# Two edits of order in a hybrid streaming encoder: the PSUM bank of the small columns, and what VectorE and ScalarE do first in the merge

## Chip, cores and metric

The kernel runs on one core of a Trainium2 chip. The metric is the time of one execution on the device, in microseconds, as the median of several runs. The profile is of one further execution.

## The reference, cut to what matters

Two layers of an encoder for 512 prompt frames and 64 sample frames (T = 576 columns), width 1024, float32. Each layer is a token mixer and a gated MLP with a short convolution; what the change touches is the mixer:

```python
(a_q, a_k, a_v, i_q, i_k, i_w, b_q, b_k, b_v, c_q, c_k, c_v, c_f) = jnp.split(xn @ w_in, points, axis=-1)
c_logf = jax.nn.log_sigmoid(c_f + b_f)
# three attentions: A sparse (indexer i_q, i_k, i_w picks keys), B stick-breaking, C forgetting (c_logf)
branch = jnp.einsum('btnw,nwd->btnd', o, w_branch)
gate = jax.nn.sigmoid((xn @ w_gate).reshape(B, T, N_BRANCH, D_MODEL))
return jnp.einsum('btnd,btnd->btd', gate, branch) @ w_out
```

The "small columns" are a_v (64), i_w (4) and c_f (8): 76 columns of the projection that are narrower than a tile and go together.

## The kernel before, in words

Activations lie transposed: 128 features on the partitions, 576 frames in the free dimension, eight such tiles for the width of 1024. Each operand of a product is split in a high and a low part (wh and wl of the weights, xh and xl of the activations), and a product is three matmuls (high-high, high-low, low-high) for each half of 288 frames. One output tile over 1024 inputs is 48 matmuls.

Weights come in units of 512 KB into two raw buffers. A unit is two chunks of 512 columns. For each chunk ScalarE makes the high part (`high_part`, L455) and VectorE the low part (`low_part`, L798), into one of four slots. A high part waits until TensorE has finished the chunk four before it (semaphore `chunks`), TensorE waits for the low part (`low_done`), and SyncE loads the next unit when both low parts of a unit are made.

Output tiles go in turn to two PSUM buffers of two banks each, `dbank[0]` and `dbank[1]` (called bank 0 and bank 1 here). Each use has a number `d`; its bank is `d % 2`. TensorE begins use d when `dfree[d % 2]` says that the use before it in that bank has been taken out by VectorE. The uses at the start of a layer are D_KI = 0 (keys of branch A and of the indexer), D_IQ0 = 1 (index query, first tile; the second goes to another PSUM tensor, `ab`), D_SMALL = 2, and D_PASSED = 3, a use without a product, which TensorE marks as done itself so that the next use, D_Q[B] = 4, falls in bank 0. Nothing is planned at run time: each engine has a list of instructions in the order in which its Python code writes them, and runs it in that order.

TensorE's order at the start of a layer (L1477 on) is: keys, index query 0, index query 1, small columns (L1488), first half of query tile 0 of branch B (L1491), five transposes of the small columns (L1497), second half of that query tile (L1499), first half of the next (L1500), eight small products for the forget logits (L1505, L1506), second half (L1507), and then the index heads (L1517). VectorE's order is: take the keys (L818), take index query 0 (L820), low part 8, take index query 1 (L956), copies for the samples, low part 9, rotate the keys (L829 to L832), copy them (L965), low part 10, take the small columns (L969), copy a row of rstd into them (L971, which frees the bank), low part 11, rotate index query 0, low part 12, extract the turned small columns (L979 to L986), take query tile 0 (L820), and on to the forget logits (L995, L996). ScalarE makes the high parts and four partition-shifting copies for each rotation (L461).

The merge follows each branch's attention, in the order B, C, A (so six times in two layers). TensorE multiplies the branch's output o (split in oh and ol) by w_branch, eight tiles j = 0 to 7 in turn in the two banks. `branch_first` (L1425) does tiles 0 and 1, interleaved so that the high products of both come ahead of the low ones: the last 8 matmuls of tile 0, then the rest of tile 1, whose last 8 matmuls end it. Tiles 2 to 7 go through `dense` (L1370). VectorE multiplies tile j by gate j (L1216 in branch B, L1218 in C and A), which frees the bank, and in C and A adds the result to z (L1220). The gates are made by ScalarE and VectorE during the attention: VectorE takes the projection (L904), ScalarE makes abs, exp and ln (`gate_ln`), VectorE subtracts (`gate_sub`, L909), ScalarE makes the final exp (`gate_exp`, L494). The eighth gate (number 7) is finished at the start of the merge.

Of the kernel before, what the change touches and what calls it, by code (L numbers as in the profile page):

```python
# [40 lines left out]
HEADS = 8  # L41
# [16 lines left out]
B, C, A = 0, 1, 2  # L58
# [4 lines left out]
U_BR = {B: 24, C: 48, A: 64}  # L63
# [7 lines left out]
RAW_SLOTS = 2  # L71


D_KI, D_IQ0, D_SMALL, D_PASSED = range(4)
D_Q = {B: 4, C: 37, A: 70}
D_V = {B: 8, C: 41}
D_K = {B: 9, C: 42}
# [56 lines left out]
def encoder(nc, xT, w, const, masks, par, ki_past, v_past, bc_k_past, bc_v_past, lf_past,  # L134
            y, o_ki, o_k, o_v, o_av, o_lf, o_conv):
    with ExitStack() as ctx:
# [85 lines left out]
        def sem(name):  # L222
            return ctx.enter_context(nc.semaphore(name))
# [7 lines left out]
        dfree = [sem("dfree0"), sem("dfree1")]  # L231
# [30 lines left out]
        def chunks_done(l, n):  # L262

            return l * CHUNKS + SPLIT_SLOTS + n

        def freed(l, d):

            return START + l * (D_USES // 2) + d // 2
# [5 lines left out]
        def wait_taken(eng, l, d):  # L274

            eng.wait_ge(dfree[d % 2], freed(l, d) + 1)
# [155 lines left out]
        def _(act):  # L432
# [3 lines left out]
            def high_parts(l, upto, at_chunk=None):  # L436

                while split[0] <= upto:
                    c = split[0]
                    high_part(l * CHUNKS, l * (UNITS // 2), c)  # L440
                    split[0] += 1

            def high_part(before, units_before, c, in_half=0):
                v_ = c // 2
                if c % 2 == 0:

                    act.wait_ge(landed[v_ % 2], 16 * (units_before + v_ // 2 + 1))

                act.wait_ge(chunks, before + c + 1)
                stored = raw[v_ % 2][:, (c % 2) * 512:(c % 2) * 512 + 512]  # L450
                if v_ + in_half in TURNED_UNITS:
                    act.activation(as_turned(wh[:, c % SPLIT_SLOTS, :], 0), as_stored(stored, 0), ACT.Copy)
                    act.activation(as_turned(wh[:, c % SPLIT_SLOTS, :], 1), as_stored(stored, 1), ACT.Copy).then_inc(high_done, 1)
                else:
                    act.activation(wh[:, c % SPLIT_SLOTS, :], stored, ACT.Copy).then_inc(high_done, 1)  # L455
# [18 lines left out]
            def round_z(l, kk):  # L474

                act.wait_ge(z_ready, l * KD + kk + 1)
                act.activation(xh[:, kk, :], z[:, kk, :], ACT.Copy).then_inc(xh_ready, 1)

            def gate_ln(l, m, h):

                wait_taken(act, l, D_G[m] + 2 * h)
                part = tmp[:]
                act.activation(part, g[:, h, :], ACT.Abs).then_inc(act_steps, 1)
                steps[0] += 1
                act.wait_ge(act_steps, l * ACT_STRIDE + steps[0])
                act.activation(part, part, ACT.Exp, scale=-1.0).then_inc(act_steps, 1)
                steps[0] += 1
                act.wait_ge(act_steps, l * ACT_STRIDE + steps[0])
                act.activation(part, part, ACT.Ln, bias=1.0).then_inc(gate_lns, 1)

            def gate_exp(l, m, h):

                act.wait_ge(gate_subs, l * 24 + 8 * m + h + 1)
                act.activation(g[:, h, :], g[:, h, :], ACT.Exp).then_inc(gates_ready, 1)  # L494
# [14 lines left out]
            for l in range(LAYERS):  # L509
# [31 lines left out]
                for m in (B, C, A):  # L541
# [157 lines left out]
                        gate_exp(l, m, 2 * p)  # L699
                    high_parts(l, cg + 7)  # L700
                    gate_ln(l, m, HEADS - 1)
                    gate_exp(l, m, HEADS - 1)

                    for j in range(KD):

                        high_parts(l, 2 * U_BR[m] + j + 4)
                        if m == A and j:
                            round_z(l, j - 1)

# [67 lines left out]
        def _(dve):  # L777
# [4 lines left out]
            def step(ins):  # L782

                ins.then_inc(dve_steps, 1)
                steps[0] += 1
# [4 lines left out]
            def low_part(before, c, in_half=0):  # L790
                dve.wait_ge(high_done, before + c + 1)
                stored = raw[(c // 2) % 2][:, (c % 2) * 512:(c % 2) * 512 + 512]
                highs, lows = wh[:, c % SPLIT_SLOTS, :].bitcast(F32), wl[:, c % SPLIT_SLOTS, :]
                if c // 2 + in_half in TURNED_UNITS:
                    dve.tensor_tensor(as_turned(lows, 0), as_stored(stored, 0), as_turned(highs, 0), ALU.subtract)
                    dve.tensor_tensor(as_turned(lows, 1), as_stored(stored, 1), as_turned(highs, 1), ALU.subtract).then_inc(low_done, 1)
                else:
                    dve.tensor_tensor(lows, stored, highs, ALU.subtract).then_inc(low_done, 1)  # L798

            def low_parts(l, upto):  # L800
                while split[0] <= upto:
                    low_part(l * CHUNKS, split[0])
                    split[0] += 1
# [86 lines left out]
            def split_low(l, m, p):  # L890

                dve.wait_ge(oh_ready, l * 12 + 4 * m + p + 1)
                dve.tensor_tensor(ol[:, p, :], q[:, p, :], oh[:, p, :].bitcast(F32), ALU.subtract).then_inc(ol_ready, 1)  # L893
# [12 lines left out]
            def gate_sub(l, m, h):  # L906

                dve.wait_ge(gate_lns, l * 24 + 8 * m + h + 1)
                dve.scalar_tensor_tensor(g[:, h, :], g[:, h, :], 0.0, tmp[:], ALU.min, ALU.subtract).then_inc(gate_subs, 1)  # L909
# [36 lines left out]
            for l in range(LAYERS):  # L946
# [95 lines left out]
                for m in (B, C, A):  # L1042
# [162 lines left out]
                        for p in range(PAIRS - 1):  # L1205
                            split_low(l, m, p)
                    split_low(l, m, PAIRS - 1)
                    gate_sub(l, m, HEADS - 1)

                    for j in range(KD):  # L1210
                        low_parts(l, 2 * U_BR[m] + j + 4)
                        d = D_BR[m] + j
                        dve.wait_ge(chunks, chunks_done(l, 2 * U_BR[m] + j + 1))
                        dve.wait_ge(gates_ready, l * 24 + 8 * m + j + 1)
                        if m == B:
                            dve.tensor_tensor(z[:, j, :], dv[d % 2], g[:, j, :], ALU.mult).then_inc(dfree[d % 2], 1)  # L1216
                        else:
                            dve.tensor_tensor(g[:, j, :], dv[d % 2], g[:, j, :], ALU.mult).then_inc(dfree[d % 2], 1)  # L1218
                            dve.wait_ge(dfree[d % 2], freed(l, d) + 1)
                            ins = dve.tensor_tensor(z[:, j, :], z[:, j, :], g[:, j, :], ALU.add)  # L1220
                            if m == A:
                                ins.then_inc(z_ready, 1)
                                if j % 2:
                                    low_x(l, 1, j - 1)
                            else:
                                step(ins)
# [130 lines left out]
        def _(pe):  # L1357
            def dense(before, lo_wait, c0, outs, rh, rl, kks, begin=True, end=True):

                for n, kk in enumerate(kks):  # L1360
                    c = c0 + n // 4
                    if n % 4 == 0:

                        pe.wait_ge(low_done, before + c + 1)
                    lo_wait(kk)
                    a = (n % 4) * P
                    hi_w, lo_w = wh[:, c % SPLIT_SLOTS, a:a + P], wl[:, c % SPLIT_SLOTS, a:a + P]
                    for w_, r_, first, last in ((hi_w, rh, True, False), (hi_w, rl, False, False), (lo_w, rh, False, True)):
                        for half in range(2):
                            ins = pe.matmul(outs[half], w_, r_[:, kk, HALF * half:HALF * half + HALF],  # L1370
                                            start=first and n == 0 and begin, stop=last and n == len(kks) - 1 and end)
                    if n % 4 == 3 or n == len(kks) - 1:
                        ins.then_inc(chunks, 1)
# [23 lines left out]
            def project(l, u, d, wait=no_wait):  # L1397
                pe.wait_ge(dfree[d % 2], freed(l, d))
                dense(l * CHUNKS, wait, 2 * u, dhalf[d % 2], xh, xl, range(KD))
# [77 lines left out]
            for l in range(LAYERS):  # L1477
                project(l, U_KI, D_KI, xn_wait(l, 0))
                project(l, U_IQ, D_IQ0)
                if l == 0:  # L1480
                    dense(l * CHUNKS, no_wait, 2 * (U_IQ + 1), iq1_out, xh, xl, range(4), True, False)
                    pe.wait_ge(s_const, 16)
                    norm_sum(1)
                    dense(l * CHUNKS, no_wait, 2 * (U_IQ + 1) + 1, iq1_out, xh, xl, range(4, KD), False, True)
                else:
                    norm_sum(1 + 2 * l)
                    dense(l * CHUNKS, no_wait, 2 * (U_IQ + 1), iq1_out, xh, xl, range(KD))
                project(l, U_SMALL, D_SMALL)  # L1488
                wait_taken(pe, l, D_IQ0)
                pe.sem_inc(dfree[D_PASSED % 2], 1)  # L1490
                project_half(l, U_Q[B], D_Q[B], 0)  # L1491

                wait_taken(pe, l, D_SMALL)
# [539 lines left out]
```

## Time and profile before

| | |
|---|---|
| median of 3 runs | 2167.99 us (2167.51 to 2168.78) |
| the profiled execution | 2157.28 us |
| its span | 2155.4 us |
| TensorE busy | 2125.5 us, 99% |
| TensorE's weight loads busy | 2012.8 us, 93% |
| VectorE busy | 1341.5 us, 62% |
| ScalarE busy | 992.1 us, 46% |
| GpSimd busy | 187.8 us, 9% |
| mean granted TensorE clock | 0.997 of full speed |
| mean DMA rate | 81 GB/s |

The span goes from the first instruction to the last; the execution's own time has a little more around it. Busy times of one engine are the union of its instructions; matmuls are pipelined, so one lasts longer than the distance to the next. L971 is line 971 of the kernel before.

### The profile page before, as it was taken

To read this page: it belongs to the slowest core of one execution; us is meant where nothing else is said; L and a number is where in the kernel's file an instruction comes from. 1 tells how busy PE (TensorE), PEld (TensorE's weight loads), DVE (VectorE), ACT (ScalarE), POOL (GpSimd) and SP (SyncE) were. 2 spreads that over 40 slices of the span, in tenths; PEclk is the share of its full clock that TensorE was granted. 3 is DMA by queue.
4 is the path that set the end of the run, shared out by engine and by line. 5 is a ranking of instruction groups with operands and counts; after the bars stand their busy time and mean duration, and the time that the engine had idled before them with its cause. 6 is when DMAs were issued, how large, how long until landed. Compare 5 with 4: busy or idle time off the path is not lost.

```text
span 2155.4 us, 40042 instructions
## 1 busy us (share of the span) xinstructions
PE 2125.5 (99%) x16142; PEld 2012.8 (93%) x16142; DVE 1341.5 (62%) x2537; ACT 992.1 (46%) x1611; POOL 187.8 (9%) x138
## 2 busy tenths in 40 slices
PE   7999999999999999999999999999999999999998
PEld 7898998898899999999988989888989999999998
DVE  6668646766556773566465785377766476536653
ACT  5347414646626652344342672255465366424431
POOL 0000000000031110011300100000000301001112
PEclk9999999999999999999999999999999999999999
DMA  5231223121122222222232212231211222222222
GB/s 186 77 104 40 72 85 113 40 79 50 50 80 88 79 87 91 86 88 88 89 105 78 94 40 94 73 99 53 71 50 60 79 88 79 88 89 78 88 80 94
DMA packets 53493, 175.06 MB, mean 81 GB/s; under 512 B 6705, under 2 KB 11393, under 8 KB 53361
## 3 DMA queue, kind: packets, MB, share of 16 engines
q1 hardware_dynamic: 46896, 158.88, 23.9%
q0 software_dynamic: 2688, 9.95, 1.2%
q10 hardware_dynamic: 3776, 4.34, 0.6%
q8 instruction: 99, 1.62, 0.3%
q14 instruction: 34, 0.27, 0.0%
HBM read 160.25 MB, written 12.90 MB: 80 GB/s over the span
## 4 chain that ended last, share of the span: by engine, by line
PE 94%; DVE 3%; ACT 2%; issue 1%; DMA 0%; ACTq 0%; SPq 0%; DVEq 0%
PE d L1370 61%; PE d L1420 14%; PE ab L1466 4%; PE ab L1698 2%; PE d L1750 2%; PE d L1741 2%; PE d L1611 1%; PE d L1470 1%; PE ab L1691 1%; PE ab L1728 1%; DVE ol L893 1%; PE d L1431 0%; PE ab L1517 0%; PE d L1864 0%; PE ab L1548 0%
## 5 line engine op out<-in xcount | busy, mean ns | idle before, releaser
L455 ACT ACTIVATE wh<-raw 128x512 fp32r<-128x512 f32 x548 | 345.1, 631 | 736.9 <-PE d L1370 611.2
L798 DVE TENSOR_TENSOR wl<-raw,wh 128x512 fp32r<-128x512 f32 x548 | 379.9, 695 | 367.3 <-ACT wh L455 358.5
L1370 PE MATMUL d<-xh,wh 128*128 128x288 f32 x2400 | 517.4, 296 | 16.9 <-DVE z L971 8.5
L1370 PE MATMUL d<-xl,wh 128*128 128x288 f32 x2400 | 514.7, 295 | 0.0
L1370 PE MATMUL d<-xh,wl 128*128 128x288 f32 x2400 | 514.4, 295 | 0.0
L1370 PEld LDWEIGHTS d<-xh,wh 128*128 128x128 f32 x2400 | 385.8, 189 | 20.9 <-issue 10.6
L1370 PEld LDWEIGHTS d<-xl,wh 128*128 128x128 f32 x2400 | 385.7, 189 | 0.0
L1370 PEld LDWEIGHTS d<-xh,wl 128*128 128x128 f32 x2400 | 385.7, 189 | 0.0
L1420 PE MATMUL d<-xh,wh 128*128 128x288 f32 x768 | 173.3, 307 | 0.5 <-DVE g L904 0.5
L1420 PE MATMUL d<-xh,wl 128*128 128x288 f32 x768 | 164.5, 295 | 0.0
L1420 PE MATMUL d<-xl,wh 128*128 128x288 f32 x768 | 164.4, 295 | 0.0
L1370 PE MATMUL d<-al,wh 128*128 128x288 f32 x682 | 145.4, 294 | 0.0
L1370 PE MATMUL d<-ah,wh 128*128 128x288 f32 x682 | 145.3, 294 | 0.0
L1370 PE MATMUL d<-ah,wl 128*128 128x288 f32 x682 | 145.3, 294 | 0.0
L1420 PEld LDWEIGHTS d<-xh,wh 128*128 128x128 f32 x768 | 122.3, 189 | 3.9 <-DVE g L904 1.0
L1420 PEld LDWEIGHTS d<-xl,wh 128*128 128x128 f32 x768 | 123.2, 188 | 0.0
L1420 PEld LDWEIGHTS d<-xh,wl 128*128 128x128 f32 x768 | 123.0, 188 | 0.0
L410 POOL TENSOR_TENSOR al<-at,ah 128x576 f32 x44 | 63.9, 1451 | 652.6 <-ACT ah L740 652.6
L1274 DVE TENSOR_TENSOR hb<-d,rstd 128x512 f32<-128x512 f32 x88 | 60.9, 692 | 88.8 <-PE d L1370 88.8
L1370 PEld LDWEIGHTS d<-ah,wh 128*128 128x128 f32 x682 | 108.9, 188 | 0.0
L1370 PEld LDWEIGHTS d<-ah,wl 128*128 128x128 f32 x682 | 108.9, 188 | 0.0
L1370 PEld LDWEIGHTS d<-al,wh 128*128 128x128 f32 x682 | 108.8, 188 | 0.0
(319 smaller groups left out, 3236.4 us busy)
## 6 DMA issues: line engine op xcount, KB each, us to landing
raw<-in_w SPq DMA_DIRECT2D x288, 512.0 KB, 3.5
out_o_k<-k POOLq DMA_DIRECT2D x4, 1152.0 KB, 7.3
out_o_v<-v POOLq DMA_DIRECT2D x4, 1024.0 KB, 8.9
x<-in_xT SPq DMA_DIRECT2D x8, 288.0 KB, 6.6
out_y<-z SPq DMA_DIRECT2D x16, 144.0 KB, 1.9
k<-in_bc_k_past ACTq DMA_DIRECT2D x4, 512.0 KB, 5.0
v<-in_bc_v_past ACTq DMA_DIRECT2D x4, 512.0 KB, 6.2
w<-in_masks SPq DMA_DIRECT2D x1, 800.0 KB, 6.5
```

Of the source, the lines that this page charges most:

```text
L410: pool.tensor_tensor(al[:, bass.ds(i, 1), :].rearrange("p a n -> p (a n)"), at[:], ah[:, bass.ds(i, 1), :].rearrange("p a n -> p (a n)").b ...
L455: act.activation(wh[:, c % SPLIT_SLOTS, :], stored, ACT.Copy).then_inc(high_done, 1)
L798: dve.tensor_tensor(lows, stored, highs, ALU.subtract).then_inc(low_done, 1)
L893: dve.tensor_tensor(ol[:, p, :], q[:, p, :], oh[:, p, :].bitcast(F32), ALU.subtract).then_inc(ol_ready, 1)
L1274: dve.tensor_tensor(hb[:, s, 2:514], hv[:, 0:512], rstd[:, 0:512], ALU.mult)
L1370: ins = pe.matmul(outs[half], w_, r_[:, kk, HALF * half:HALF * half + HALF], start=first and n == 0 and begin, stop=last and n == len(kks) ...
L1420: ins = pe.matmul(dhalf[d][half], w_, r_[:, kk, HALF * half:HALF * half + HALF], start=first and kk == 0, stop=last and kk == KD - 1)
L1466: pe.matmul(o, x_[:, kk, t * P:t * P + P], w_[:, c % SPLIT_SLOTS, cols:cols + n], start=first and f_ and starts(t), stop=last and l_, skip ...
L1470: ins = pe.matmul(src(4), xp[:, kk, :], w_[:, c % SPLIT_SLOTS, cols:cols + n], start=first and f_ and starts(4), stop=last and l_, skip_gr ...
L1698: pe.matmul(ab[:, bank + i, a:a + n], q[r, p, t * P:(t + 1) * P], keys(r, p)[:, 0:n], start=a == 0, stop=False, skip_group_check=True)
L1741: ins = pe.transpose(spare[:, o + n:o + n + P], w1[:, a + n:a + n + P], ident)
L1750: pe.matmul(spare[r, t * P:(t + 1) * P], val(2 * p + i, kt), w2[:, w:w + P], start=first, stop=kt == t, skip_group_check=True)
```

## The change

Two things. D_SMALL and D_PASSED change places, so that the small columns go to bank 1 and the passed use is in bank 0; TensorE marks the passed use ahead of the small columns, when the keys have been taken (use 0, bank 0). In the merge, VectorE multiplies tile j by its gate ahead of low part j + 4 instead of behind it. The subtraction for gate 7 moves behind the product of tile 0 (VectorE), and the exponential for gate 7 moves behind the first high part of the merge (ScalarE). No instruction is added or taken away.

```diff
-D_KI, D_IQ0, D_SMALL, D_PASSED = range(4)
+D_KI, D_IQ0, D_PASSED, D_SMALL = range(4)
@@ ScalarE
                     gate_ln(l, m, HEADS - 1)
-                    gate_exp(l, m, HEADS - 1)
 
                     for j in range(KD):
 
                         high_parts(l, 2 * U_BR[m] + j + 4)
+                        if j == 0:
+                            gate_exp(l, m, HEADS - 1)
                         if m == A and j:
                             round_z(l, j - 1)
@@ VectorE
                     split_low(l, m, PAIRS - 1)
-                    gate_sub(l, m, HEADS - 1)
 
                     for j in range(KD):
-                        low_parts(l, 2 * U_BR[m] + j + 4)
                         d = D_BR[m] + j
                         dve.wait_ge(chunks, chunks_done(l, 2 * U_BR[m] + j + 1))
                         dve.wait_ge(gates_ready, l * 24 + 8 * m + j + 1)
@@ 
                             dve.tensor_tensor(z[:, j, :], dv[d % 2], g[:, j, :], ALU.mult).then_inc(dfree[d % 2], 1)
                         else:
                             dve.tensor_tensor(g[:, j, :], dv[d % 2], g[:, j, :], ALU.mult).then_inc(dfree[d % 2], 1)
+                        if j == 0:
+                            gate_sub(l, m, HEADS - 1)
+                        low_parts(l, 2 * U_BR[m] + j + 4)
+                        if m != B:
                             dve.wait_ge(dfree[d % 2], freed(l, d) + 1)
                             ins = dve.tensor_tensor(z[:, j, :], z[:, j, :], g[:, j, :], ALU.add)
@@ TensorE
+                wait_taken(pe, l, D_KI)
+                pe.sem_inc(dfree[D_PASSED % 2], 1)
                 project(l, U_SMALL, D_SMALL)
-                wait_taken(pe, l, D_IQ0)
-                pe.sem_inc(dfree[D_PASSED % 2], 1)
                 project_half(l, U_Q[B], D_Q[B], 0)
```

## Rows read from the trace of the kernel before

**Rows 1.** The page, busy time, share of the span and instructions of each engine.
```profile
PE 2125.5 (99%) x16142; PEld 2012.8 (93%) x16142; DVE 1341.5 (62%) x2537; ACT 992.1 (46%) x1611; POOL 187.8 (9%) x138
```
**Rows 2.** TensorE's waits: waiting line, releasing line, total us, times, longest.
```profile
PE d L1370 <- DVE z L971: 8.5, 2, 6.3
...
PE d L1370 <- DVE g L1218: 2.6, 4, 0.7
PE d L1370 <- DVE z L1216: 1.5, 2, 0.7
```
**Rows 3.** The chain that ended last, one half projection: start us, us, what.
```profile
23.99 3.20 PE ab L1370 x24
```
**Rows 4.** Timeline of TensorE, layer 0: start us, us, instructions [idle before, releaser].
```profile
31.11 0.42 PE L1370 MATMUL d<-xh,wh 128*128 128x288 f32 x2
...
37.09 0.42 PE L1370 MATMUL d<-xh,wl 128*128 128x288 f32 x2
...
43.77 0.85 PE L1370 MATMUL d<-xh,wh 128*128 128x288 f32 x2 [6.25 <-DVE z L971]
...
49.04 0.58 PE L1497 MATMUL ab<-cf,z 97*128 97x97 f32 x5
...
60.51 1.77 PE L1517 MATMUL ab<-k,iq 64*128 64x512 f32 x8
```
**Rows 5.** Timeline of VectorE in the same stretch.
```profile
30.36 0.75 DVE L820 SCALAR_TENSOR_TENSOR iq<-d,rstd 128x576 f32<-128x576 f32 x1
...
43.26 0.46 DVE L971 COPY z<-rstd 1x576 f32<-1x576 f32 x1
...
50.30 0.69 DVE L798 TENSOR_TENSOR wl<-raw,wh 128x512 fp32r<-128x512 f32 x1 [3.74 <-ACT wh L455]
...
58.45 0.26 DVE L996 TENSOR_SCALAR z<-ab,pr 8x64 f32<-8x64 f32 x1
```
**Rows 6.** Windows: stretch, length, busy of PE, PEld, DVE, ACT, POOL, granted clock, DMA, GB/s.
```profile
40.50:41.50 1.00, 0.00 (x0) 0.00 (x0) 0.97 (x3) 0.98 (x3) 0.00 (x0) 0.94 0.13 49
...
47.50:48.50 1.00, 1.00 (x6) 1.00 (x6) 0.00 (x0) 0.00 (x0) 0.00 (x0) 0.64 0.04 16
...
2148.00:2149.00 1.00, 0.21 (x1) 0.00 (x0) 0.69 (x2) 0.72 (x2) 0.00 (x0) 1.00 0.30 106
...
2150.00:2151.00 1.00, 0.00 (x0) 0.00 (x0) 1.00 (x4) 0.00 (x0) 0.00 (x0) 0.91 0.46 164
```
**Rows 7.** Timeline around line 971 in layer 1.
```profile
1101.76 0.43 PE L1370 MATMUL d<-xh,wl 128*128 128x288 f32 x2
...
1103.89 0.46 DVE L971 COPY z<-rstd 1x576 f32<-1x576 f32 x1
...
1104.40 0.53 PE L1370 MATMUL d<-xh,wh 128*128 128x288 f32 x2 [2.22 <-DVE z L971]
```
**Rows 8.** Timeline of ScalarE in layer 0, the high part of chunk 12.
```profile
49.64 0.63 ACT L455 ACTIVATE wh<-raw 128x512 fp32r<-128x512 f32 x1 [7.08 <-PE d L1370]
```
**Rows 9.** Timeline of two merges in layer 0, branch B and, from 590, branch A.
```profile
242.60 1.23 PE L1431 MATMUL d<-ol,wh 128*128 128x288 f32 x8
...
243.51 0.69 ACT L494 ACTIVATE g<-g 128x576 f32<-128x576 f32 x1 [2.94 <-DVE g L909]
...
244.20 1.23 PE L1431 MATMUL d<-ol,wh 128*128 128x288 f32 x8
...
244.75 0.69 DVE L798 TENSOR_TENSOR wl<-raw,wh 128x512 fp32r<-128x512 f32 x1 [1.27 <-ACT wh L455]
...
245.36 0.75 DVE L1216 TENSOR_TENSOR z<-d,g 128x576 f32<-128x576 f32 x1
...
246.16 0.53 PE L1370 MATMUL d<-oh,wh 128*128 128x288 f32 x2 [0.73 <-DVE z L1216]
...
590.53 1.23 PE L1431 MATMUL d<-ol,wh 128*128 128x288 f32 x8
...
592.33 0.53 PE L1370 MATMUL d<-oh,wh 128*128 128x288 f32 x2 [0.57 <-DVE g L1218]
```

## The prediction

> **What bounds the kernel now.** I read the page first, and there the busy line: TensorE runs for 99% of the span, VectorE 62%, ScalarE 46% [rows 1]. So a wait is worth only what TensorE itself stands still. The second view is who waited for whom on TensorE. It has three rows of interest [rows 2]: 8.5 us in two waits for VectorE's line 971 (the longest 6.3), 2.6 us in four waits for line 1218, 1.5 us in two waits for line 1216. These are the two places that the change touches: the small columns once in each layer, and the third tile of each of the six merges. The third view is the timeline around each. Everything between is TensorE work back to back, which a change of order doesn't touch: half a projection, 24 products, takes 3.20 us [rows 3], so 0.133 us a product.
>
> **Part 1, the bank of the small columns.** In layer 0 the last products of the small columns start at 37.09, and the next (query tile 0 of branch B, in the same bank 0) at 43.77, after 6.25 us of idle time [rows 4]. Its bank comes free when VectorE has done line 971, 43.26 + 0.46 = 43.72 [rows 5]. VectorE isn't waiting for TensorE there: it works off its own list (the query's and key's rotations, copies, low parts), so the 43.72 doesn't move. With the small columns in bank 1, the half projection finds bank 0 free (its earlier user, the index keys, was taken ahead of line 820, which starts at 30.36 [rows 5]) and runs from about 37.4 to 40.7. Its weights, chunk 8, were split long before. Then TensorE waits for the same 43.72, since the transposes read what line 971 writes, and starts them at 43.77 instead of 49.04 [rows 4]: 5.27 us, which is 3.2 us of half projection moved ahead of the wait and 2.07 us of clock. For the half projection took 5.27 us where 24 products want 3.20: the granted clock had fallen (0.94 in 40.5 to 41.5, 0.64 in 47.5 to 48.5 while it rose again [rows 6]), from 2.4 to 1.2 GHz.
>
> Does the clock stay up now? TensorE still stands from 40.7 to 43.77, 3.0 us. Before, the clock fell at about 41.4 (0.94 over the slice is 88% of it at full clock), 3.9 us behind the last product at 37.5. At the end of the kernel it fell at about 2150.8 (0.91 is 82% of the slice), only 2.6 us behind the last matmul, which ended at 2148.2, but with other gaps ahead of that [rows 6]. In layer 1 a stop of 2.2 us cost no clock: the next products came at their usual pace [rows 7]. 3.0 us lies between. I take "stays up" because the one long gap that follows dense work took 3.9 us, and this is dense work too; the other answer is a rival. Price of a fall: the part behind the stop runs at half rate for about as long as it did, so about 2.1 us.
> The Trainium skill (TensorE: Matmul & The Clock Gate, Part 1) says that the gate's window runs free of the kernel, so the same kernel can come out either way from run to run; it calls for a whole idle window, and the fall at the kernel's end here, soon after work, shows that this needn't be taken strictly. By its rule this gap would keep the clock, which is the forecast above.
>
> Two waits are added or moved. The small columns now need line 820's result taken (30.36 + 0.75 = 31.11), and they started at 31.11 [rows 4, 5]: 0.1 to 0.3 us late in layer 0, but what follows ends in the stop before 43.72 anyway, so nothing. Behind that wait only TensorE's own queue stands. The wait for the index query that stood behind the small columns is gone from there; the wait for the index keys now ahead of them is long met.
>
> What is late next? TensorE comes 5.2 us earlier to everything behind the transposes, VectorE less. VectorE's next step was low part 12 at 50.30, after 3.74 us of idle time for ScalarE's high part [rows 5], and that one ran at 49.64 because TensorE had to give up chunk 8 [rows 8]. Chunk 8 is now done at 40.7, the high part follows the one before it on ScalarE at about 42.6, so VectorE goes straight on at about 46.5: 3.7 us earlier. The check that counts, because its slack is the smallest in this list: the forget logits (line 996) done at 58.45 + 0.26 - 3.7 = 55.0, TensorE's index heads want it at 60.51 - 5.2 = 55.3 [rows 4, 5]. The slack is 0.3 us, small but there. If it breaks it costs at most the difference of the two moves, 5.2 - 3.7 = 1.5 us. Bounds of layer 0: from 3.1 (clock falls) less 1.5, so 1.6, to 5.3. I take 5.2.
>
> Layer 1: the last small products start at 1101.76, two of them, so the next could start at 1102.03; they started at 1104.40 [rows 7]. The half projection now fills 1102.03 to 1105.2, and line 971 is done at 1103.89 + 0.46 = 1104.35 [rows 7], so nothing is left of the stop: 2.37 us. The first pair after a stop takes 0.53 instead of 0.43 us [rows 7], and that 0.1 goes too: 2.5 us. Bounds 1.5 (if VectorE's list is late next) to 2.5. Part 1: 5.2 + 2.5 = 7.7 us.
>
> **Part 2, the merge.** In the merge of branch B, layer 0, TensorE ends the second tile with 8 products from 244.20 (the next could start 8 x 0.133 later, at 245.27) and starts the third at 246.16 [rows 9]. It waits for its bank, which VectorE frees with the product by the gate: 245.36 + 0.75. That product was queued behind low part 4 (244.75), which waited for ScalarE's high part, which stood behind the exponential of the last gate (243.51 + 0.69) [rows 9]. The tile itself was done at 242.60 + 1.23 = 243.83 [rows 9]. With the product first on VectorE it runs from about 243.9 to 244.65: 0.6 us ahead of TensorE's 245.27. The stop goes whole: 246.16 - 245.27 = 0.89, and 0.1 of restart. In branch A it is 592.33 - (590.53 + 1.07) = 0.73, and 0.1 [rows 9]. The four B and C merges are alike (2.6 and 1.5 us over the six rows' waits agree with it: 0.7 each [rows 2]). Sum: 4 x 0.99 + 2 x 0.83 = 5.6 us. Bounds: 4.1 us (the waits as the view has them) to 5.6 us; 0 if the product comes no earlier (a rival).
>
> What the edit puts later: gate 7's subtraction starts at about 244.65 and its exponential on ScalarE at about 245.4, high part 5 right behind it at about 246.1 instead of 245.5. Gate 7 is wanted at the eighth tile, 15 us on; chunk 5 at the sixth tile, more than 9 us on. Low part 4 is done by 246, wanted at 251.7. In the other steps VectorE multiplies first and splits then; either way bank and chunk are ready well within TensorE's 3.2 us a tile. Nothing here touches a DMA beyond moving its trigger by under a microsecond: raw slots are filled one unit ahead, and TensorE has no wait for one past the start. Cost 0, cover lost only if VectorE's step grew over 3.2 us.
>
> **Sum.** 7.7 + 5.6 = 13.3 us off a span of 2155.4 (execution 2157.28). The time outside the span stays, so 2144.0 for a profiled execution. The median of the runs shown, 2167.99, is 10.7 us above the profiled execution, and I carry that over unchanged: 2167.99 - 13.3 = 2154.7 us, 0.6% faster. What a measurement of this kernel can tell from no change is about 0.2%, 4.3 us.
>
> **Rivals.**
> (a) The clock falls in the 3.0 us left in layer 0. For: at the end it fell 2.6 us behind the last matmul. Against: 3.9 us in this same place. Gain 13.3 - 2.1 = 11.2: 2156.8 us.
> (b) VectorE's or ScalarE's list becomes the bound behind the transposes, the slack of 0.3 us being eaten, or the clock effect and this together. Gain 13.3 - 1.5 to 13.3 - 3.6: 2156 to 2158.5 us.
> (c) The merge edit doesn't do what it says: the product finds its tile marked done no earlier than the low part was ready. Against it: ScalarE's high part 5 started at once when tile 1's last product ended. Gain 7.7: 2160.3 us.
> (d) Slower: the merges become bound by VectorE. A step of branches C and A holds a low part (0.69), a product (0.75), a sum and in every other step of A a low half of z, about as long: 2.2 to 3.0 us [rows 9]. Past 3.2 us a step TensorE would wait at each tile. At 0.5 us over in the 32 steps of C and A it costs 16 us and gives 13.3 - 5.6 less, so 7.7 - 16: 8 us slower, 2176 us. It decides at 3.2 us; the rows are under it and the edit adds no work, so it is nearly excluded.
>
> **Chances.** Forecast 0.50, (a) 0.27, (b) 0.10, (c) 0.08, (d) 0.02, and 0.03 for a gain under 4.3 us by something not seen. Range 2153.0 to 2159.5: below for up to 1.5 us more from restarts and clock, above over (a) and (b). Faster by over 0.2%: 0.94; within 0.2%: 0.04; slower: 0.02.
>
> **What would show it.** In the trace after: no wait of TensorE for line 1216 or its fellow in the other branches; one wait for line 971, in layer 0, of about 3.0 us, none in layer 1; the transposes right behind it; granted clock 1.00 in the 5 us behind (half if (a)); VectorE's idle time ahead of low part 12 gone. The prediction is wrong if TensorE shows a new wait for lines 996, 986 or 820 (b), or the third tile's wait stays (c).

## The result, and the profile after

The changed kernel took 2135.13 us (median of 6 runs, 2133.7 to 2135.8); the kernel before beside it 2162.49 us (6 runs). The ratio is 0.9888, with a 95% interval from 0.9858 to 0.9917. The forecast was 2154.7 us, in a range from 2153.0 to 2159.5: right in sign, and its 13.3 us are half of the 27.4 us between the two medians.

The median of before hides something that the rest of this document is about: its six runs lie at two levels, three at 2167.5 to 2168.8 us and three at 2156.6 to 2157.5. The profiled execution (2157.28 us) is one of the lower level. The changed kernel has one level.

The page after, and TensorE's waits after (columns as in [rows 1, 2]; the changed kernel's lines are up to three further down: 1373 is 1370 of before, 972 is 971, 1215 and 1217 are 1216 and 1218):
```profile
span 2133.9 us, 40042 instructions
...
PE 2113.4 (99%) x16142; PEld 2002.3 (94%) x16142; DVE 1338.5 (63%) x2537; ACT 991.7 (46%) x1611; POOL 191.5 (9%) x138
```
```profile
PE d L1373 <- DVE wl L797: 8.6, 1, 8.6
PE ab L1500 <- DVE z L972: 3.1, 1, 3.1
```
The first row is the wait for the first weights. All six waits of the merges are gone, and of the two for the small columns one is left, in layer 0. So the waits went as forecast. But TensorE's busy time fell too, by 12.1 us (2125.5 [rows 1] to 2113.4), with the same 16142 instructions. Shorter waits don't do that.

The left wait and what it did to the clock, in the timeline and the windows after (columns as in [rows 4, 6]):
```profile
39.59 0.43 PE L1373 MATMUL d<-xh,wl 128*128 128x288 f32 x2
...
43.10 1.07 PE L1500 MATMUL ab<-cf,z 97*128 97x97 f32 x5 [3.09 <-DVE z L972]
```
```profile
42.00:43.00 1.00, 0.00 (x0) 0.00 (x0) 0.97 (x2) 0.41 (x1) 0.00 (x0) 0.70 0.00 0
...
48.50:49.50 1.00, 1.00 (x7) 1.00 (x6) 0.00 (x0) 0.00 (x0) 0.84 (x1) 0.63 0.00 0
```
The half projection runs up to 40.0, ahead of the wait as planned, and the granted clock falls all the same, at about 42.4 (0.70 over the slice is 40% of it at 2.4 GHz), 2.4 us behind the last product. It comes back at about 49.2 (0.63 over the slice is 26% of it at 2.4 GHz), 6.1 us after the restart. This was rival (a).

The merge of branch B in layer 0, VectorE and then TensorE, beside [rows 9]:
```profile
240.74 0.76 DVE L1215 TENSOR_TENSOR z<-d,g 128x576 f32<-128x576 f32 x1 [1.06 <-PE d L1434]
241.41 0.75 DVE L910 SCALAR_TENSOR_TENSOR g<-g,tmp 128x576 f32<-128x576 f32 x1
242.08 0.68 DVE L799 TENSOR_TENSOR wl<-raw,wh 128x512 fp32r<-128x512 f32 x1
```
```profile
241.07 1.23 PE L1434 MATMUL d<-ol,wh 128*128 128x288 f32 x8
242.14 0.43 PE L1373 MATMUL d<-oh,wh 128*128 128x288 f32 x2
```
VectorE's product frees the bank at 241.5, TensorE wants it at 242.14 and goes on without a gap: 0.6 us of slack, as forecast.

Where the 21.5 us of the span went shows best in the chain that ended last, where long stretches of TensorE stand as one row. The two rows that matter are the MLP of layer 0 and of layer 1 (start, us, what). Before:
```profile
592.33 77.04 PE d L1370 x576
670.34 418.08 PE d L1370 x3216
...
1729.02 407.19 PE d L1370 x3054
```
After:
```profile
586.65 76.80 PE d L1373 x576
664.42 418.08 PE d L1373 x3216
...
1717.74 397.02 PE d L1373 x3054
```
At the start of layer 1's MLP the changed kernel is 1729.02 - 1717.74 = 11.3 us ahead. Its end brings 10.17 more: 3054 products in 397.02 us, 130.0 ns each, where the kernel before took 407.19, 133.3 ns each. Layer 0's 3216 products ran at 130.0 in both traces (418.08). The granted clock is 1.00 in all of it and TensorE never stands.

Each product's start in the trace shows what the two paces are. At 133.3 the distances are 131, 131, 131, 140 ns, over and over; at 130.0 they are 128 and 132 in turn. In the MLP and in the merge and projection ahead of it, the pace changes at one place only: the four float32 matmuls of the norm sum (L1380, the sum of squares for the next norm, started 242 ns apart) behind the first MLP tile. Distances in ns ahead of the sum, the last one being that to the sum itself | and behind it, past the first four (worked out from the starts in the traces):
```
before, layer 0   140 131 131 132 140 130 131 132 | 132 128 132 128    130.0 from here on
before, layer 1   131 132 140 131 131 131 140 132 | 131 132 140 130    133.3
after,  layer 0   140 131 131 132 140 130 131 132 | 132 128 132 128    130.0
after,  layer 1   140 130 131 132 140 131 131 131 | 131 129 131 129    130.0
```
In the slow case the sum comes one product behind the 140, in the others three behind it. Where this place comes from can be read too. In the kernel before, TensorE restarts in the merge of branch A 576 products ahead of the sum, which is a multiple of four; of the distances behind that restart the first 140 is the 13th in layer 0 and the 7th in layer 1, so the two cycles lie two products apart from there on. That was the theory for the experiments, **theory P**: the place in this cycle at which the norm sum comes decides the pace of the whole MLP, and TensorE's last stop ahead of it sets the place.

### The profile page after: what moved, and what is told of

It reads as the page before. It is cut to its first block, busy times and chain, and to the rows that moved or that the text cites. A ratio compares the mean times of both kernels' runs of the same rounds, so it can differ in the third digit from the quotient of the medians.

```text
span 2133.9 us, 40042 instructions
## 1 busy us (share of the span) xinstructions
PE 2113.4 (99%) x16142; PEld 2002.3 (94%) x16142; DVE 1338.5 (63%) x2537; ACT 991.7 (46%) x1611; POOL 191.5 (9%) x138
## 4 chain that ended last, share of the span: by engine, by line
PE 96%; DVE 2%; ACT 1%; DMA 0%; issue 0%; ACTq 0%; SPq 0%; DVEq 0%
PE d L1373 61%; PE d L1423 14%; PE ab L1469 4%; PE d L1434 2%; PE ab L1701 2%; PE d L1753 2%; PE d L1744 2%; PE d L1614 1%; PE d L1473 1%; PE ab L1694 1%; PE ab L1731 1%; PE ab L1373 0%; PE ab L1520 0%; PE d L1867 0%; PE ab L1551 0%; PE d L1568 0%
## 5 line engine op out<-in xcount | busy, mean ns | idle before, releaser
L1373 PEld LDWEIGHTS d<-xh,wh 128*128 128x128 f32 x2400 | 384.1, 189 | 12.1 <-issue 10.7
L1288 DVE SCALAR_TENSOR_TENSOR cv<-hb,pr,cv 128x578 f32<-128x578 f32 x88 | 72.3, 821 | 58.0 <-ACT cv L732 58.0
```

The source lines that it names most:

```text
L1288: dve.scalar_tensor_tensor(cv[:, s, :], hb[:, s, 1:T + 3], pr[:, bass.ds(R_CW + CONV * row + 1, 1)], cv[:, s, :], ALU.mult, ALU.add).then_ ...
```

## The experiments

Twelve kernels in three groups (e1 to e4, e5 to e8, e9 to e12), each with its own runs of the kernel before.

**e1, e2: one part each.** e1 has the first and the last block of the diff, e2 the blocks between.

> Only part 1 (the small columns in the other bank); the merge as before. The profiles of before and after show two paces of the 288-column products: 130.0 ns each, or 133.3 ns (131, 131, 131, 140 over and over). The MLP of layer 1 ran at 133.3 before (the chain has 407 us for 3054 products) and at 130.0 after (397 us): 10.2 us of the 21.5 us that the span fell. Theory P (phase): TensorE's pace is one of two locks; the norm sum inside the first MLP tile pair is where it may change, and whether it does hangs on the place in the cycle of four at which the sum comes, which the last stop of TensorE ahead of it sets, that is the stop in the merge of branch A. Part 1 leaves that stop, so layer 1 should stay at 133.3 (or change by the chance of the stop's nanoseconds): span 2155.4 less 5.7 (part 1 as the two traces have it: 3.1 and 2.5), about 2149.7; 2139.5 if the stop's nanoseconds fall otherwise. Rival R: the pace is drawn anew for each execution or each load of a program, whatever the instructions: layer 1 and layer 0 at either pace, span 2139.5, 2149.7 or 2160. Rival A (mine from before): the change is only the sum of its stops, and the 10 us come from somewhere in part 1.

> Only part 2 (the order in the merge); the small columns in bank 0 as before. Stops in the merge gone in all six, so 5.6 us. Theory P: with no stop in the merge of layer 1's branch A the norm sum comes at the same place of the cycle as in the changed kernel, so layer 1's MLP runs at 130.0 ns a product: span about 2133.9 + 5.7 = 2139.6, 15.8 below before. Rival R: 2139.6, 2149.8 or 2160, by chance. Rival A: 2149.8.

e1 took 2161.06 us (6 runs, 2160.8 to 2162.2), ratio 0.9965 (0.9952 to 0.9977); e2 took 2141.53 us (4 runs, 2141.3 to 2141.9), ratio 0.9873 (0.9857 to 0.9890). The kernel before ran sixteen times beside them: fifteen at 2166.7 to 2171.4, one at 2158.7. The MLP rows of the chain, e1:
```profile
665.85 428.80 PE d L1370 x3216
...
1732.51 407.19 PE d L1370 x3054
```
and e2:
```profile
666.48 418.08 PE d L1373 x3216
...
1723.80 397.02 PE d L1373 x3054
```
With the merge's stops left in, both MLPs run at 133.3 (428.80 and 407.19); without them, both at 130.0. e1's level I had missed, since layer 0 was slow too, which the profile of before had not shown. The small part of the change, by its stops, is worth the large part of the gain. Rival A had the 10 us come from part 1; it is out. Against the before of their group (2168.69 us) part 1 alone gives 7.6 us, close to the 7.7 forecast for it, and part 2 alone 27.2 where its stops were forecast at 5.6. The pace makes up the rest.

**e3, e4: two thrown-away products ahead of layer 1's norm sum.**
```diff
                         up(f, 0, 0, xn_wait(l, 2))
+                        for r in range(2 if l else 0):
+                            pe.matmul(iq1_out[0], ntri, xh[:, 7, 0:HALF], start=True, stop=True)
                         norm_sum(2 + 2 * l)
```


> The kernel before with two more 288-column products in layer 1 (constant weights by the last tile of xh, into an unused bank, result thrown away), issued by TensorE between the first MLP tile and the norm sum. Before, the norm sum there came right behind the long (140 ns) product of the cycle, after: two products later. Theory P: with two more it comes as in the changed kernel, and the MLP of layer 1 runs at 130.0: 10.2 less 0.3 us, span about 2145.5. Rival R: no relation, 2155.7 or any of the levels 10 us apart. If the pace were set by other engines' accesses, 2155.7 too.

> The changed kernel with the same two thrown-away products ahead of layer 1's norm sum. Theory P: the norm sum comes two places later in the cycle, right behind the 140 ns product as in the kernel before, and layer 1's MLP falls back to 133.3: span 2133.9 + 0.3 + 10.2 = 2144.4. Rival R and any cause in the other engines: 2134.2, or any level by chance.

e4 took 2145.66 us (4 runs, 2145.4 to 2146.4): beside the changed kernel's 2135.13 it loses 10.5 us by 0.26 us of work, and the chain has 407.19 for layer 1, as theory P had it. e3 took 2168.03 us (10 runs, one of them 2158.2), no gain: its layer 1 too is at 133.3. The distances ahead of its sum were 140 131 131 131 140 134 132 129. This is a miss that counts: the sum stood three behind a 140, the place of the fast case, and the pace stayed slow. The added products, with weights of their own, don't continue the cycle (134 132 129 where it has 131 131 131 or the like; e4 has 131 130 135 135), so they may break it rather than move the place by two; but then e4's hit isn't clean evidence for the place either. It shows that two products ahead of the sum can cost the pace. e7 and e8 move the sum without adding anything.

**e5, e6: the new order in the merges of branch A alone, or everywhere but there.** In each of the three places the edit is made conditional, as in VectorE's part of e5 (e6 has `m != A`):
```diff
+                        if not (m == A):
+                            low_parts(l, 2 * U_BR[m] + j + 4)
                         d = D_BR[m] + j
```


> The kernel before with the new order in the merges of branch A alone (two of six); bank and the other four merges as before. In the job before this one the kernel before ran mostly at 2168.7 us and once at 2158.7 (sixteen runs), the bank change alone at 2161.1, the merge change alone at 2141.5, and the profiles say that the merge change alone had both MLPs at 130.0 ns a product and the bank change alone both at 133.3. Theory P: TensorE's last stop ahead of each MLP, the one in the merge of branch A, sets the place in the cycle of four at which the norm sum comes; without it both MLPs run at 130.0. Then: 2168.7 less 1.7 for the two stops and 20.9 for the pace (6270 products x 3.33 ns), 2146.1 us. Rival M: the pace hangs on all stops of the mixer, those of B and C too, so most of it stays: 2167 or 2157. Rival R (drawn by chance at each run): several levels 10 us apart within the runs.

> The changed kernel with the old order in the merges of branch A alone. Theory P: the stops of 0.8 us come back, and with them the place at which the norm sum comes is the one of the kernel before: mostly 133.3 ns in both MLPs: 2135.1 + 1.7 + 20.9 = 2157.7 us, at times 2147. Rival M: both stay at 130.0, 2136.8.

e5 took 2145.93 us (4 runs, 2143.8 to 2146.3; expected 2146.1), ratio 0.9892 (0.9876 to 0.9909), beside a before of 2168.49 us (7 runs, all of the upper level). e6 took 2157.92 us (4 runs, 2157.9 to 2159.4; expected 2157.7), ratio 0.9953 (0.9936 to 0.9970). e6's MLP rows:
```profile
664.85 428.80 PE d L1379 x3216
...
1729.71 407.19 PE d L1379 x3054
```
Two stops of 0.8 us, taken out, give 22.6 us; put back, they cost 22.8 us (against the changed kernel's 2135.13 us, which was not run again beside e6). Rival M (all stops of the mixer count) is out.

**e7, e8: the norm sum six products later, nothing added.** Six is two places in a cycle of four.
```diff
-                        norm_sum(2 + 2 * l)
-                        up(f, 0, 1)
+                        up(f, 0, 1, behind_first=lambda: norm_sum(2 + 2 * l))
```
(`dense` calls `behind_first` after its first block of six products.)

> The kernel before; only TensorE issues the norm sum of both MLPs six products later (behind the first block of the second tile). Six is two places in the cycle of four, and no product is added. Theory P: where the sum came right behind the 140 ns product (133.3 ns afterwards, the usual case of the kernel before) it now comes two places later, as in the changed kernel, and both MLPs run at 130.0: 2168.7 - 20.9 = 2147.8 us. Where it came in the other place before (the rarer case) it would now be slow. Rival R and causes in other engines: 2168.7. A theory by which the pace is a matter of the stops themselves, not of the place of the sum: 2168.7.

> The changed kernel with the norm sums six products later in the same way. Theory P: the sum comes right behind the 140 ns product in both layers and both MLPs run at 133.3: 2135.1 + 20.9 = 2156.0 us, in all runs. Rivals: 2135.1.

e7 took 2147.72 us (5 runs; four at 2147.1 to 2147.7, expected 2147.8, one at 2158.0), ratio 0.9903 (0.9887 to 0.9920). e8 took 2155.94 us (4 runs, 2155.4 to 2156.2; expected 2156.0), ratio 0.9941 (0.9925 to 0.9958). e8, the changed kernel with its sums later:
```profile
664.73 427.99 PE d L1373 x3210
...
1728.45 406.39 PE d L1373 x3048
```
The same edit makes the one kernel 20.8 us faster and the other 20.8 us slower. The profile of e7 is of the run at 2158.0, with one layer at each pace: 140 132 ahead of the sum in layer 0 (133.3 behind it), 140 130 131 132 in layer 1 (130.0). That is the rare case of before, turned round. The rivals (the stops' own length, other engines, chance in each run) had no change to forecast from this edit.

**e9: the stop that is left in layer 0.** In layer 0 alone VectorE takes the small columns sooner:
```diff
                 low_parts(l, 9)
+                if l == 0: take_small()          # L969 to L971
...                                               # rotate and copy the keys, low parts 10 and 11
+                if l == 0: extract()              # L976 to L986, ahead of rope(l, 1, ...)
...
+                if l == 0: constants(); logits()  # L993 to L996, ahead of low part 13 and rope(l, 2, ...)
```


> The changed kernel; in layer 0 VectorE takes the small columns ahead of the rotation of the keys, extracts the turned columns ahead of the rotation of the index query, and makes the forget logits ahead of low part 13 and the last rotation. It tests my rival (a): the stop of 3.1 us left in layer 0, and the half clock behind it (2.3 us over 48 products, 0.6 us over the transposes and what follows), are one thing. With the stop gone the granted clock should stay at 1.00 in the whole of 37 to 60 us, and TensorE should come to the index heads about 3.1 + 2.9 = 6 us earlier, at about 51.5, where VectorE's list (logits at about 51.6) is as late: so 5.5 to 6 us, 2129.5 us, with both MLPs still at 130.0. If the clock fell for another reason, the half-rate stretch stays and the gain is 3.1 us or less, 2132.

e9 took 2130.70 us (6 runs, 2130.0 to 2132.2), ratio 0.9850 (0.9820 to 0.9879), 4.4 us under the changed kernel's median: the fastest version of all. Its windows over the stretch:
```profile
37.00:41.00 4.00, 4.00 (x33) 4.00 (x32) 3.82 (x7) 3.92 (x6) 0.00 (x0) 1.00 0.47 137
41.00:45.00 4.00, 4.00 (x34) 4.00 (x33) 3.88 (x9) 2.34 (x5) 0.00 (x0) 1.00 0.01 2
45.00:49.00 4.00, 4.00 (x32) 3.39 (x32) 3.87 (x12) 0.88 (x2) 1.45 (x2) 1.00 0.54 168
```
TensorE stands nowhere in this stretch and the clock stays at 2.4 GHz. The span fell by 5.0 us (2133.9 to 2128.9). This profile had reached the transposes, by then without a wait, about 0.9 us later than the changed kernel ended its half projection, so between these two profiles the stop with its clock was worth 5.9 us, of 5.5 to 6 expected.

By the medians it is 4.4 us, 1.2 short of the forecast, and the other traces show a reason. The transposes and the 48 products behind them take 6.92 us in e9, at full clock. In the seven traces that have the stop they take 9.73 and 9.63 us in two (the changed kernel, e10), and 8.32 to 8.52 in five (e1, e4, e6, e8, e11). So the clock fell behind this stop every time, but it cost 2.8 us in some executions and about 1.5 in others. The stop and the cheaper fall make 4.6 us.

**e10, e11: can the rest of the mixer be put on the faster pace?** The merges and the output projection run at 133.3 in every trace up to here. Two float32 matmuls like the sum's behind the third tile of merge A:
```diff
+                        if m == A and j == 2:
+                            for half in range(2):   # 32 columns in e11
+                                pe.matmul(iq1_out[half], cf[:, C_ONE:C_ONE + P], cf[:, C_COS:C_COS + 288], start=True, stop=True)
```


> The changed kernel with two float32 matmuls like the norm sum's (288 columns, constants, result thrown away) behind the third tile of the merges of branch A, in both layers. The third tile begins at the same place of the cycle as the norm sum (tiles are 48 or 24 products, multiples of four). Theory P: from there on the rest of the merge and the output projection (504 products a layer) run at 130.0 instead of 133.3: 1.7 us less for 1.0 us of added work, and the norm sum then comes in the fast cycle, of which I know nothing: if it keeps, 2135.1 - 1.4 = 2133.7; if it breaks, 2154.6. If only a real norm sum in the MLP did it: 2137.1.

> As e10 with 32 columns instead of 288 in the added matmuls, so 0.3 us a layer or less. Theory P: if the pace may change wherever other matmuls come between the 288-column ones at the right place, the rest of the merge and the output projection run at 130.0: 2135.1 - 2.8 = 2132.3, or +20.9 if the norm sum breaks it. If the length of the added ones matters, the pace stays at 133.3 up to the norm sum, and what follows may go either way.

No. e10 took 2158.20 us (10 runs, 2156.4 to 2159.8), e11 2156.93 (10 runs, 2156.7 to 2157.4). The added matmuls came three products behind the 140 in all four merges, the right place, and still the merge and the output projection stayed at 133.3; the norm sum then came one product behind the 140 in both layers: both MLPs at 133.3 (428.80 and 407.19). So 0.3 us of work a layer cost 21.8 us. Theory P held for the MLP and failed for its extension: at this place in the program, the right place in the cycle was not enough. What else it takes is open.

**e12: the kernel before once more.**

> The kernel before once more, to see in a profile what its usual time (2168.7) is made of. Theory P: both MLPs at 133.3 ns a product (428.8 us for the 3216 products in layer 0 and 407.2 for the 3054 in layer 1), the norm sums right behind the 140 ns product in both layers. If it is the rare case (2157 to 2158) again, one of the two at 130.0.

It ran at 2156.71 us, the rare level again, beside 23 timed runs of before of which 18 lay at 2167.1 to 2171.0 and 5 at 2156.6 to 2158.3. Its chain:
```profile
669.85 418.08 PE d L1370 x3216
...
1728.45 407.19 PE d L1370 x3054
```
The lower level has one slow MLP, as in the first profile. The upper level (43 of all 52 timed runs of before) was not caught in a profile of before itself. The nearest is e3's, an execution of 2167.36 us of a kernel that differs only by its two products in layer 1: 428.80 and 407.19, both slow. Beside it stand e1 and e6, which keep the stop of merge A, e7's 20.8 us, and the distance of 10.7 us to the lower level, which is layer 0's 428.80 - 418.08.

Over all profiles, the sum in the MLP came three products behind the 140 eleven times, counting only kernels without added matmuls, and 130.0 followed each time; it came one behind it nine times (and four more in e10 and e11), and 133.3 followed each time.

Two further norm sums in every kernel bear this out, though no experiment was aimed at them. The one in the first projections of layer 0 (at 26 to 28 us) came three behind the 140 in eight of the fourteen traces, with the fast rhythm right behind it, and one behind it in six, with the slow one. The one at the start of layer 1 came in the slow rhythm in seven, and the place decided again: e8, three behind, and the changed kernel, where the MLP before it was fast:
```profile
1093.68 6.24 PE ab L1373 x48
```
```profile
1083.47 6.39 PE ab L1373 x48
```
The first is 130.0 ns a product, the second 133.1: in the changed kernel the sum came in the fast rhythm and ended it, as in all seven traces where it came so.

## Why the prediction was wrong, step by step

**The step that failed** stands in the first paragraph: "Everything between is TensorE work back to back, which a change of order doesn't touch", with 0.133 us a product as if it were a constant. It isn't: the same product is started every 133.3 or every 130.0 ns, 6270 products hang on it in the two MLPs, and the edit touched it by taking out the stop ahead of them (e2, e5, e6). Layer 1's share is 10.2 us in the pair of profiles; against before's usual level it is both layers', 20.9 us. The profile of before showed it, unread: the chain had 418.08 us for 3216 products and 407.19 for 3054, 130.0 and 133.3.

**The offset.** I carried the 10.7 us between the profiled execution and the median over as time outside the span. Every execution has 1.8 to 2.5 us outside its span (2157.28 - 2155.4, 2135.80 - 2133.9). By all that the runs show, the 10.7 us were layer 0's MLP at the slower pace. A median that lies 10.7 us off a profiled run, where runs agree within 1.3 us, should have been a question.

**Part 1, layer 1:** right. From the chain, the kernels lie 5.92 us apart at the MLP of layer 0 and 1108.27 - 1099.88 = 8.39 behind the transposes of layer 1: 2.5 us, forecast 2.5. That the stop of 2.2 us in layer 1 cost no clock is true of the trace of before, but not of every one: in layer 1 of e2, e3 and e7, which keep the small columns in bank 0, the clock fell just behind the restart from the same stop of 2.2 to 2.5 us, and the half projection took 4.8 us instead of 3.3.

**Part 1, layer 0:** the order was right and the clock wrong. I gave "the clock stays up" 0.50 and (a) 0.27; it fell in this profile. At the first product behind the forget logits (57.14 us before, 54.01 after) the changed kernel is 3.1 us ahead, of which 1.0 us is from the first products of the kernel, where the clock rose sooner in this run (96 products in 14.44 instead of 15.53 us; 14.3 to 15.7 over the profiles). So 2.1 us instead of the 5.2 forecast or the 3.1 of (a). A size was off in (a) too: I took the price of a fall as the 2.1 us of before; it was 2.3 us in the 48 products behind the transposes (8.73 us against 6.41) and 0.5 in the transposes, since the clock came back only 6.1 us after the restart (4.4 before). In the five traces with the cheaper fall it was about 1.5 in all.

Part 1 as a whole, by e1's medians, gave 7.6 us where 7.7 was forecast. That is luck in part: the forecast had the clock stay up, and in e1's trace it fell.

As to the gate, the Trainium skill (TensorE: Matmul & The Clock Gate, Part 1) calls for an idle window; here the clock fell 2.4 us behind the last product, in a stop of 3.1 us, and rival (a), not the page's reading that I took as support, was right. The measurement decides: with a stop of 2.5 us (e6) it fell as well, 1.0 us after TensorE had restarted.

**What is late next:** right. VectorE went straight on with low part 12 at 45.81 and TensorE waited for nothing on the way to the index heads. Rival (b) did not come in.

**Part 2:** right in mechanism and size. The steps between the kernels in the chain are 0.98, 0.99 and 0.82 us for the merges B, C, A of layer 0 and 0.98, 0.99 and 0.92 in layer 1, 5.7 us, forecast 5.6. Rivals (c) and (d) are out: the waits are gone, and no new one came.

Sum by profile: 1.0 (start) + 2.1 + 2.5 + 5.7 = 11.3, and 10.2 for the pace, 21.5 us. Between the medians of before's usual level and of the changed kernel it is about 33.5 us, of which the pace is 20.9.

## What to carry to other kernels

Divide long rows of the chain by their counts before calling TensorE's work fixed: two stretches of the same product at 130.0 and 133.3 ns are a finding of the size of any wait. Where runs of a kernel lie at levels, ask which stretch makes the distance, and which level the profile is of; a profile and a median of different levels don't belong in one sum. A short stop can cost far more than it lasts, by the clock behind it (3.1 us and 1.5 to 2.8 more) or by where it leaves TensorE's rhythm (0.8 us and 10), so the gain of taking it out is read from the next long stretch, not from the wait.

## What the runs showed of the hardware that was not expected

TensorE, fed with these 288-column matmuls and a weight load for each, has two steady rhythms at the same clock of 2.4 GHz: distances of 131, 131, 131, 140 ns (mean 133.3) and of 128 and 132 in turn (mean 130.0). In the MLPs it stays in one for 3000 products, through waits that are met in time and through loops. Four slower matmuls (242 ns apart) took it from the first rhythm to the second if they came three products behind a 140, and not if they came one behind it, at three norm sums of the program; coming in the second rhythm, they took it back to the first (seven of seven). This isn't the only way in: every trace has 96 products at 130.0 behind 512-column matmuls, without a norm sum. Before:
```profile
106.27 12.48 PE d L1370 x96
```
Why the place decides, and why like matmuls in the merge (e10) and a sum behind a disturbed cycle (e3) did not do it, stays open.

By its single level of times, the place at the sum seems to be the same in every run of the changed kernel, and in the kernel before it varies from run to run. There it goes with the restart behind the stop of merge A: its first distances differ between the two layers of one trace, as shown above. What makes one restart differ from another was not tried.
